# A decoder step's retention layer: states, heads and gates in one order, weight rests on VectorE

## The reference

```python
q, k, v, g = split(x @ w_in)                    # 12 units of 512 columns: q, q, k, k, 4 x v, 4 x g
inner = einsum('bihd,bjhd->bhij', q, k) * dmask
o = einsum('bhij,bjhv->bihv', inner, v) + einsum('bihd,bhdv->bihv', q, state) * cross_decay
new_state = chunk_decay * state + einsum('bjhd,bjhv->bhdv', k * k_decay, v)
y = (silu(g) * normalised(o) * gain) @ w_out    # normalised over the 512 values of a head
```

## Time and profile before

| | |
|---|---|
| median of three runs | 1302.49 us (1297.64 to 1302.97) |
| profiled execution | 1305.03 us, span 1303.2 us |
| mean granted clock | 0.925 |
| TensorE busy | 1145.6 us, 88% |
| VectorE busy | 614.9 us, 47% |
| ACT busy | 319.0 us, 24% |
| GpSimd busy | 239.1 us, 18% |
| weight rests on GpSimd | 198.0 us, 22 of 9004 ns |
| memory | 319.67 MB, mean 245 GB/s |

### The profile page before, as it was taken

How to read it: one execution, slowest core, us unless ns; L and a number is a source line. 1 busy time by engine, 2 the same in 40 slices (tenths; PEclk the granted TensorE clock), 3 DMA queues, 4 the chain that set the end, 5 groups by cost and what they waited for, 6 DMA issues and landing times.

```text
span 1303.2 us, 14242 instructions
## 1 busy us (share of the span) xinstructions
PE 1145.6 (88%) x5410; PEld 683.5 (52%) x5410; DVE 614.9 (47%) x1092; ACT 319.0 (24%) x512; POOL 239.1 (18%) x92
## 2 busy tenths in 40 slices
PE   4989989889879999995999999599879689998992
PEld 3867656544544343432778833257668554343431
DVE  2676738562622232226699167636631713222235
ACT  3234325430311111112344200333340411111111
POOL 5526300000000000002556301315544000000000
PEclk9889995998789999998899999899989689999997
DMA  9132245185629999984233399753235849999961
GB/s 298 68 130 85 98 181 202 46 302 201 257 102 430 425 429 428 427 351 181 99 129 130 129 322 398 271 202 124 71 129 201 347 169 428 427 429 429 428 267 41
DMA packets 62537, 319.67 MB, mean 245 GB/s; under 512 B 4674, under 2 KB 4706, under 8 KB 50066
## 3 DMA queue, kind: packets, MB, share of 16 engines
q1 hardware_dynamic: 54162, 288.93, 56.4%
q0 software_dynamic: 8032, 28.79, 5.9%
q10 hardware_dynamic: 288, 1.20, 0.3%
HBM read 296.02 MB, written 22.89 MB: 245 GB/s over the span
## 4 chain that ended last, share of the span: by engine, by line
PE 71%; DVE 14%; DMA 8%; issue 3%; ACT 3%; SPq 0%; DVEq 0%; POOL 0%; ACTq 0%; POOLq 0%
PE bank L1064 24%; PE bank L904 15%; PE bank L933 7%; DMA ring<-in_w_exp_up 6%; PE bank L1310 4%; PE bank L871 3%; DVE arena L2236 2%; PE bank L883 1%; PE bank L1160 1%; PE bank L1091 1%; PE bank L1187 1%; PE bank L1041 1%; DMA ring<-in_w_in_attn 1%; DVE arena L1859 1%; PE bank L884 1%
## 5 line engine op out<-in xcount | busy, mean ns | idle before, releaser
L634 POOL TENSOR_TENSOR ring_parts<-ring,ring_parts 128x4096 fp32r<-128x4096 f32 x22 | 198.0, 9004 | 418.5 <-ACT ring_parts L629 418.4
L1064 PE MATMUL bank<-ring_parts,XTt_parts 128*128 128x512 f32 (+1 forms) x624 | 202.5, 404 | 7.8 <-DVE ring_parts L1932 6.1
L1064 PE MATMUL bank<-ring_parts 128*128 128x512 f32 x616 | 197.5, 398 | 0.0
L904 PE MATMUL bank<-ring,XTt 128*64 128x512 f32 x768 | 169.5, 598 | 12.5 <-DMA ring<-in_w_exp_up 10.6
L1064 PEld LDWEIGHTS bank<-ring_parts,XTt_parts 128*128 128x128 f32 x624 | 120.0, 196 | 36.1 <-issue 9.9
L1064 PEld LDWEIGHTS bank<-ring_parts 128*128 128x128 f32 x616 | 117.8, 193 | 25.9 <-issue 1.5
L904 PEld LDWEIGHTS bank<-ring,XTt 128*64 128x64 f32 x768 | 56.9, 138 | 122.0 <-issue 106.2
L933 PE MATMUL bank<-ring,arena 128*64 128x512 f32 x512 | 116.6, 609 | 0.0
L1784 DVE TENSOR_TENSOR arena<-XTt,bank 128x512 f32<-128x512 f32 x16 | 17.2, 1075 | 209.3 <-PE bank L904 209.3
L629 ACT ACTIVATE ring_parts<-ring 128x4096 fp32r<-128x4096 f32 (+1 forms) x24 | 83.3, 3474 | 82.1 <-DMA ring<-in_w_in_ret 76.0
L1859 DVE TENSOR_TENSOR arena<-arena 128x512 f32<-128x512 f32 (+3 forms) x30 | 66.3, 2210 | 41.0 <-ACT arena L1465 33.4
(11 more groups left out here) (257 smaller groups left out, 1367.2 us busy)
## 6 DMA issues: line engine op xcount, KB each, us to landing
ring<-in_w_exp_down SPq DMA_DIRECT2D x32, 2048.0 KB, 12.9
ring<-in_w_exp_up SPq DMA_DIRECT2D x32, 2048.0 KB, 16.1
ring<-in_w_exp_gate SPq DMA_DIRECT2D x16, 2048.0 KB, 12.4
arena<-in_w_exp_gate SPq DMA_DIRECT2D x16, 2048.0 KB, 17.8
ring<-in_w_in_ret SPq DMA_DIRECT2D x12, 2048.0 KB, 7.9
ring<-in_state_ret SPq DMA_DIRECT2D x8, 2048.0 KB, 14.3
out_state_s<-ring POOLq DMA_DIRECT2D x8, 2048.0 KB, 12.6
ring<-in_w_in_attn SPq DMA_DIRECT2D x7, 2048.0 KB, 9.0
```

The source lines that it names most:

```text
L634: pool.tensor_tensor(single(weights(key)), weights(key), rounded(key), ALU.subtract).then_inc(low_ready, 1)
L904: last = pe.matmul(ps[64 * j:64 * j + 64, :], xs[:, k, x0:x0 + 64], w[:, k, :], start=(k == 0), stop=(k == KC - 1))
L1064: last = pe.matmul(ps[:, 0:width], x(t, a, k), w[c][:, k, 0:width], **at)
```

## The change

The rests of all weights move from GpSimd's program to VectorE's. The first retention unit multiplies its high part for all three tiles before its rest is awaited. States, heads and gate units are mixed: a head, then per gate unit n the three gate tiles with three states (two in the last such round) and the next head between them. ACT rounds gate unit 8 + h inside head h, ahead of the head's square root; unit 8 during unit 7. VectorE makes that rest behind the head and ahead of the round's last state. Sample keys and values are copied into rows 64 to 127 as well, the key mask covers 128 rows, and updates alternate between lower and upper rows. The slots and the order of loads change to fit; gates go to a place of their own (`SG`). The first loads of the second layer's experts come in another order.

```diff
-          + [("rin", u) for u in range(8)] + [("state", s) for s in range(NSEQ)]
-          + [("rin", u) for u in range(8, 12)] + [("rout", u) for u in range(4)]
+          + [("rin", u) for u in range(8)] + [("state", 0), ("rin", 8), ("state", 1), ("state", 2), ("state", 3)]
+          + [("rin", 9), ("state", 4), ("state", 5), ("state", 6), ("rin", 10), ("state", 7), ("rin", 11)]
+          + [("rout", u) for u in range(4)]
...
-    for s, where in enumerate((2, 0, 1, 4, 5, 2, 0, 1)):
-        load(("state", s), where)
-    for n, where, copy_at in ((8, 4, 5), (9, 2, 0), (10, 1, 4), (11, 5, 2)):
-        load(("rin", n), where)
-        rounded(("rin", n), copy_at)
+    for s in range(3):
+        load(("state", s), (2, 1, 5)[s])
+    for n, s in ((8, 3), (9, 5), (10, 7)):
+        load(("rin", n), 0)
+        rounded(("rin", n), 4)
+        for i in range(s, min(s + 2, NSEQ)):
+            load(("state", i), (2, 1, 5)[i % 3])
+    load(("rin", 11), 5)
+    rounded(("rin", 11), 2)
     held[3] = ("rin", 11)
-    for n, where, copy_at in ((0, 0, 1), (1, 4, 5), (2, 2, 3), (3, 0, 1)):
+    for n, where, copy_at in ((0, 0, 4), (1, 1, 3), (2, 5, 2), (3, 0, 4)):
         load(("rout", n), where)
         rounded(("rout", n), copy_at)
...
+    def state(s):
+        for j in range(8):
+            take(("update", s, j), ((5, 0, 1, 2) if s % 3 == 2 else (3, 4, 5, 2))[j % 4])
+    def head(h):
+        take(("inner", h), 0)
+        take(("rstate", h, 0), 1)
+        take(("rstate", h, 1), 2)
+        take(("ro", h, 0), 3)
+        take(("ro", h, 1), 4)
     take(("sinner",), 1)
     take(("so", 0), 6)
     take(("so", 1), 7)
...
-    c["ksel"] = np.where((i[:, None] // DSEQ == np.arange(NSEQ)[None, :])[:, :, None], k8, 0).reshape(128, -1)
+    c["ksel"] = np.where((i[:, None] % SAMPLE // DSEQ == np.arange(NSEQ)[None, :])[:, :, None], k8, 0).reshape(128, -1)
...
+        def update_of(j):
+            h, c = 2 * (j // 4) + j % 2, j // 2 % 2
+            return h, c, slice(64 * (j % 2), 64 * (j % 2) + 64)
...
-                        for j in ((4, 3, 1, 2, 0, 5), (4, 5, 2, 3, 0, 1))[L]:
+                        for j in ((4, 3, 1, 2, 0, 5), (1, 3, 2, 5, 0, 4))[L]:
...
-                if s == 5:
-                    low_part(pool, NIN + 8)
...
+            def store_prompt_state(h):
+                for c in range(2):
+                    wait_emptied(pool, "rstate", h, c)
+                    pool.dma_start(O["state_p"][h, c * 128:(c + 1) * 128, :], st_out[:, c, :]).then_inc(sto_stored[c], 16)
+            store_prompt_state(0)
+            for n in range(2):
+                store_state(3 * n)
+                store_state(3 * n + 1)
+                store_prompt_state(n + 1)
+                store_state(3 * n + 2)
+            store_state(6)
+            store_state(7)
+            store_prompt_state(3)
...
+            pe.wait_ge(high_ready, NIN + 1)
+            for t in range(3):
+                wait_emptied(pe, "x2", t, 0)
+                wait_emptied(pe, "x2", t, 1)
+                project(fill(("rin", 0, t)), t, x_parts, parts(("rin", 0)), stop=False, of=(0,))
...
                 for j in range(8):
-                    h, c = j // 2, j % 2
+                    h, c, own = update_of(j)
                     ps = fill(("update", s, j))
-                    pe.matmul(ps[:, :], kd[0:64, h, c * 128:(c + 1) * 128], v[0:64, 2, h, :],
+                    pe.matmul(ps[:, :], kd[own, h, c * 128:(c + 1) * 128], v[own, 2, h, :],
                               start=True, stop=True).then_inc(full(("update", s, j)), 1)
...
+            head(0)
+            for n in range(3):
+                gate(n, 0)
+                state(3 * n)
+                gate(n, 1)
+                if n == 2:
+                    state(7)
+                gate(n, 2)
+                if n < 2:
+                    state(3 * n + 1)
+                head(n + 1)
+                if n < 2:
+                    state(3 * n + 2)
+            for t in range(3):
+                gate(3, t)
+                for i in (2 * t, 2 * t + 1):
+                    turn_o(*TURNS_O[i])
+            for t in range(3):
+                turn_o(2, t)
...
+                if n == 4:
+                    act.wait_ge(rk_ready, 12)
+                    twice(kt[:, 2, :, :])
+                if n > 4:
+                    wait_emptied(act, "rin", n - 1, 2)
+                    twice(v[:, 2, n - 5, :])
+            wait_emptied(act, "rin", 7, 2)
+            twice(v[:, 2, 3, :])
+            def deviation(rows, count):
+                act.wait_ge(rvar, count)
+                act.activation(rst[:, rows, 14:15], rst[:, rows, 13:14], ACT.Sqrt, bias=epst[:, 0:1]).then_inc(rstd, 1)
+                act.wait_ge(rnmr, count)
...
+                if h:
+                    high_part(act, NIN + 8 + h)
+                deviation(slice(0, 2), h + 1)
...
+            wait_emptied(act, "sinner")
+            head(0)
+            for n in range(3):
                 for t in range(3):
...
+                    gate(n, t)
+                head(n + 1)
+            sample_outputs()
+            gate(3, 0)
+            high_part(act, NIN + 12)
+            for i in (0, 1):
+                round_gated(*TURNS_O[i])
+            gate(3, 1)
+            for i in (2, 3):
+                round_gated(*TURNS_O[i])
+            gate(3, 2)
+            for i in (4, 5):
+                round_gated(*TURNS_O[i])
             high_part(act, NIN + 13)
...
+            low_part(dve, 1)
+            low_part(dve, 2)
             rope_unit(0)
+            low_part(dve, 3)
...
+                low_part(dve, NIN + n + 1)
...
+            keys_of(0)
+            head(0)
+            for n in range(3):
+                gate(n, 0)
+                state(3 * n)
+                gate(n, 1)
+                if n == 2:
+                    state(7)
+                half(n)
+                if n < 2:
+                    state(3 * n + 1)
+                head(n + 1)
+                low_part(dve, NIN + 9 + n)
+                if n < 2:
+                    state(3 * n + 2)
+            sample_outputs()
+            for n in range(3):
+                sample_gated(n)
             dve.wait_ge(gain_in, 16)
...
+            gate(3, 0)
+            low_part(dve, NIN + 12)
+            for i in (0, 1):
+                gained(*TURNS_O[i])
+            gate(3, 1)
+            for i in (0, 1):
+                gated_low(i)
+            for i in (2, 3):
+                gained(*TURNS_O[i])
+            half(3)
+            sample_gated(3)
+            for i in range(4, 6):
+                gated_low(i - 2)
+                gained(*TURNS_O[i])
+            for i in (4, 5):
+                gated_low(i)
+            low_part(dve, NIN + 13)
+            for i in range(6, 12):
+                gained(*TURNS_O[i])
+                if i > 6:
+                    gated_low(i - 1)
...
```

More of the change, by code:

```diff
@@ L127, in last_product @@
             "rin": ("rin", u, 2), "rout": ("proj", 1, 2, u // 2)}[kind]
+TURNS_O = [(0, 0), (0, 1), (1, 0), (1, 1), (0, 2), (1, 2)] + [(n, t) for n in (2, 3) for t in range(3)]
 def psum_uses():
@@ L227, in psum_uses @@
     take(("so", 1), 7)
[L228 to L236, removed]
-    for n in range(4):
[L238 to L243, removed]
+    head(0)
+    for n in range(4):
+        take(("rin", 8 + n, 0), 0)
+        if n < 3:
+            state(3 * n)
+        take(("rin", 8 + n, 1), 1)
+        if n == 2:
+            state(7)
+        take(("rin", 8 + n, 2), 2)
+        if n < 2:
+            state(3 * n + 1)
+        if n < 3:
+            head(n + 1)
+        if n < 2:
+            state(3 * n + 2)
+    for i, (n, t) in enumerate(TURNS_O):
+        take(("oturn", n, t), 5 + i % 3)
     for u in range(2):
@@ L1264, in _ @@
                     if n == 0:
-                        wait_emptied(pe, "x2", t, 0)
-                        wait_emptied(pe, "x2", t, 1)
-                    project(fill(("rin", n, t)), t, x_parts, parts(("rin", n))).then_inc(full(("rin", n, t)), 1)
+                        project(bank[USE["rin", 0, t][0]], t, x_parts, parts(("rin", 0)), start=False, of=(1,))\
+                            .then_inc(full(("rin", 0, t)), 1)
+                    else:
+                        project(fill(("rin", n, t)), t, x_parts, parts(("rin", n))).then_inc(full(("rin", n, t)), 1)
                     if 0 < n <= 4:
@@ L1289, in _, with state @@
             last.then_inc(full(("sinner",)), 1)
[L1290 to L1291 removed]
             so = [fill(("so", g)) for g in range(2)]
[L1293 removed]
+            def state(s):
                 g = s // 4
+                if s == 0:
+                    wait_emptied(pe, "sinner")
+                    pe.wait_ge(qm_ready, 1)
                 if s % 4 == 0:
@@ L1596, in _, with head @@
                         copy(dst, ps[:, :].rearrange("p (c t) -> p c t", c=4)[:, :, 0:r]).then_inc(freed(("rturn", i, t)), 1)
-            high_part(act, NIN + 8)
-            for g in range(2):
```

(36 more changed lines are left out.)

175 lines of the change are left out of this document (86 added, 89 removed).

## The result

The changed kernel takes 1312.49 us (median of five runs, 1310.56 to 1319.05) beside 1302.49 for the kernel before: a ratio of 1.0094, 95% interval 1.006 to 1.0128. It is slower by 0.9%, more than the 0.5% that a measurement tells from no change; 1299.8 was forecast. The profiled execution took 1319.05 us (span 1317.4), 14 us more than that of before.

What follows compares the result with a forecast made beforehand. Attention and the first eight retention units were taken as TensorE-bound, the later rounds as bound by a load/store chain. 10.5 + 54.5 + 55.9 + 47.8 + 99 = 267.7 us, a -2.7 us change: 1299.8 us, range 1278 to 1314 (own 1291 to 1308).

Steps and rivals of the forecast that it cites:

- Rests on VectorE, at nothing in attention and in the first eight units: About 100 us more VectorE work, covered by TensorE's matmuls there; the norm's shorter step starts retention 1.9 us sooner.
- The halves overlap: Sample-state updates on rows 0 to 63 and 64 to 127 run at once, saving TensorE 19 us over eight states.
- the rival that had them not overlap: Updates in the two row halves don't run at once: +10 us, 1310; chance 0.05.
- Start: Last fold, sample scores and first head, ahead of the rounds: 10.5 us.
- Round 0: From gate unit 8's start, through state 0's store and unit 9's load, rounding and rest: 54.5 us.
- Round 1: The next round, through state 3's store and the next gate unit's load, rounding and rest: 55.9 us.
- Round 2: The round with two states; unit 11 lands in time but its rounding stands in head 3: 47.8 us.
- the tail: Last gates, sample outputs, turns and output product after the rounds: 99 us, with a 6 us TensorE wait.
- state 1's store begins 7 us after them and takes part of the last 3 us, 1.6 more: Round 0: this store beside the loads of state 3 and unit 9 adds 1.6 us to a 14.2 us landing.
- The slower rival: Stores and loads fight in rounds 0 and 1, +5.8 and +5.1 us: +22, 1321; chance 0.20.
- the chain: Per round: state adds, state store, state and gate-unit loads, rounding, rest, adds; round 0 lasts 54.5 us against TensorE's 42.8.
- the table load: ACT: 1.28 us each without drain, four in the chains; with the skill's 1.38 us drain, +2.8 instead of -2.7.

Runs made afterwards that it cites:

- the nine profiles: Profiled kernels, the changed one included, with the same program until the first retention unit, which starts at 619.6 to 620.6 us in four, 626.6 to 628.7 in five.
- e2: The changed kernel with all updates in rows 0 to 63 again, undoing the overlap of the halves; 1322.66 us, ratio 1.0146.
- e10: The changed kernel with only states 0, 3 and 6 stored whole, the other five cut to their first eighth; 1304.12 us, ratio 1.0017.
- e1: The changed kernel with unit 9's load issued ahead of state 3 and unit 10's ahead of state 6; 1291.27 us, ratio 0.993.
- e3: The kernel before with all weight rests moved from GpSimd to VectorE and nothing else; 1291.17 us, ratio 0.9928.
- e11: e3 plus the first retention unit's high products ahead of its rest; 1285.16 us, ratio 0.9868.
- e6: e1 plus earlier unit 11 rounding and rest, first sample-output norms, first output unit's rounding and rest, and first turned tiles; 1279.37 us, ratio 0.9825.
- e9: e6 with units 9 and 10 rounded ahead of the head's state copies and their rests made within the head; 1275.96 us, ratio 0.9789.
- e4: The changed kernel with the next gate unit rounded behind the head's scaling and its rest made behind the third state; 1307.37 us, ratio 1.0037.
- e7: The changed kernel with the rests back on GpSimd, all else as changed; 1317.78 us, ratio 1.0123.

## Why the prediction was wrong

The forecast was a small gain and the result is a small loss: the sum missed by 9.7 us in a stretch of 277. The stated range, 1278 to 1314, held the time; the forecast's own, 1291 to 1308, didn't. Step by step:

- **Rests on VectorE, at nothing in attention and in the first eight units.** Right as far as the waits go: TensorE works through all 124.85 us of the value units, and between 24 and 187 us it is busy 157.7 us, where it was 159.2 with the same products. The norm's scalings take 1.28 us each, as reckoned. Yet retention did not start 1.9 us sooner, but 3.1 later in this execution, and by the nine profiles some 4 us sooner or 3 to 5 later: the clock ahead of it outweighs this term.
- **The halves overlap.** Right, and a little larger: 22.3 us over eight states instead of 19. Undone (e2) it costs 10 us by the medians and 6.9 in the stretch; the rival that had them not overlap falls.
- **Start: 13.0 us instead of 10.5.** The fold wait of 2.9 us stands ahead of the scores, and the mean clock of the piece is 0.87. Mis-sized by 2.5.
- **Round 0: 58.1 instead of 54.5.** By links: to the store 14.6 (I had 15.1), store 9.2 (9.1), issue and landing 19.4 (16.2), rounding and scales 5.65 (5.7), rest 4.3 (4.4), the add and the updates behind it 5.0 (4.0).
- **Round 1: 60.5 instead of 55.9.** To the store 13.8 (16.5: the gate unit, which I put at half clock and 8.0, took 5.7; the half clock lay on the four updates ahead of it, in the last link of round 0), store 10.8 (9.1), issue and landing 21.0 (16.2), and 1.0 more behind the add.
- **Round 2: 45.5 instead of 47.8,** mostly for the same reason (gate unit 6.05 instead of 8.0); the tail 100.2 instead of 99, with the waits of 8.1 and 6.4 us that were named for both.

The step that failed is "state 1's store begins 7 us after them and takes part of the last 3 us, 1.6 more". By the prediction's own numbers that was already too little: a store that begins 7 us into a landing of 14.2 runs beside it for 7.2, not 3. It did begin 6.3 us after them, shared the rate for all of the 12.7 us that the second load still had to go, and two prompt-state stores of 0.25 MB joined it. At 356 GB/s, 19.0 us are 6.8 MB: the two loads of 2.1 MB each, this store and the two small ones, nearly whole. So the landing is priced by all that is moved until it ends, not by a pair and a bit for the store. e10 takes most of the stores away and the landing goes to 16.1 and 14.8, near the 14.2 that I had for a bare pair; the third load's 0.62 MB are some 1.8 us of the 16.1 (an estimate, at e10's 346 GB/s). These two links are 8.0 of the 9.7 us by which the sum missed; the rest is the start (2.5), the store of state 3 (1.7) and smaller pieces of both signs. By the medians the forecast missed by 12.7; the other 3 are outside the stretch, where the sum had nothing but the norm's 1.9. (It took 1017.3 as the end of before's stretch, 0.4 less than the earlier trace rows give.)

The slower rival had this mechanism with the price of the earlier trace rows: loads of 20.9, stores of 14.9. The loads came near it (19.0 and 20.6), the chain's own stores didn't (9.2 alone, 10.8 beside one load). It ended between the forecast and the rival.

A larger thing was not a mis-sized term, but one that I had ranked wrongly. I took the chain as given and asked how long it is; e1 cuts it by swapping two entries of the list of loads, and that alone is worth 21 us, twice what the sum missed. And the gain that the change does bring is not in its order: e3 and e11 take the kernel before to 1291 and 1285 with rests and the first unit's products alone. Only e6 and e9, with the loads swapped and each rounding and rest ahead of what it must not delay, make the mixed order pay (1279 and 1276).

On the table load: behind the rounding in round 0 ACT shows

```profile
811.82 1.28 ACT L1675 ACT_TABLE_LOAD   x1
813.11 0.30 ACT L1675 ACTIVATE arena<-arena,epst 128x2 f32<-128x2 f32 x1
```

The drain of 1.38 us that the Trainium skill's "ScalarE: Activation LUTs", section What ACT_TABLE_LOAD costs, adds to a load isn't there in the chain of the changed kernel either: the rounding ended at 811.80 us, so nothing stands ahead of the load, and the next activation follows at its end.

**What stays open.** Why the executions of one kernel scatter by 6 to 15 us (e4 from 1300.67 to 1312.01) is only partly shown: the clock between 186 and 260 us differs from one profile to the next, and with it the start of retention, but what decides it wasn't tried. Nor was it tried whether rests on VectorE change how often it falls low; the two kernels profiled with rests on GpSimd start retention at 624.0 and 622.3 us, between the two groups of the nine. The interval of a median is up to 8 us wide (e6, 0.9795 to 0.9854): the medians give e7 5 us and e9 3 us, where their rounds differ by 10 and by 8.5, and with that scatter neither contradicts. The slow clock in the start piece wasn't separated from its wait.

## What to carry over

When a chain runs through a load, price its landing as all the bytes moved until it lands, stores included, over the rate that the trace shows, and look first at what could be issued ahead of it: one swap in the list of loads was worth more than all the work that this change saved on TensorE (15.0 us of the stretch). Work taken off an engine ahead of a wait that a transfer ends comes back as a longer wait (20 of 22 us here). A rounding or rest should stand in its queue as early as its load allows (e9), neither ahead of an add that the array already waits for nor behind the whole head. Before a few us between two medians are explained, read in each trace when the edited part begins.

## What the hardware showed

- Matmuls of 64 rows on rows 0 to 63 and 64 to 127, in turn, run two at a time: 128 of them occupy 41.6 us instead of 63.9, while the mean of one is 685 ns instead of 651.
- Loads and stores share one rate: 356 and 332 GB/s with both in flight, 346 and 331 with loads and hardly any store. A 2 MB load took 8.1 us issued 1.4 us ahead of the next load and 19.0 as the second of two with a store beside it.
- While GpSimd subtracts weights, some of VectorE's operations don't end: a multiplication of two tensors on two columns took 7.05 us instead of 0.16, until the subtraction was through, while a reciprocal of one tensor beside the same subtraction took 0.17.
- The granted clock of the same instructions in the sparse part of the attention stage was 0.79 in one execution and 0.68 in another, 6 us of the time.
